# Norms by token tile, start-up transfers in pieces, and the third mixer's tables requested later, in an fp32 four-layer network on one core

## What is computed

```python
# first block: per layer
x = x + mixer(rmsnorm(x, norm_mix[i]))
x = x + ec_moe(rmsnorm(x, norm_ffn[i]))
x = rmsnorm(x, final_norm)
# second block: per layer
h = h + 0.5 * _swiglu(_rmsnorm(h, norm_ffn1[layer]), ...)
h = h + mixer(_rmsnorm(h, norm_mix[layer]), ...)
h = h + 0.5 * _swiglu(_rmsnorm(h, norm_ffn2[layer]), ...)
return _rmsnorm(h, norm_final)

def _rmsnorm(x, g):
    xf = x.astype(jnp.float32)
    y = xf * lax.rsqrt(jnp.mean(xf * xf, axis=-1, keepdims=True) + RMS_EPS)
    return (y * g.astype(jnp.float32)).astype(x.dtype)
```

## Time and profile before

| | |
|---|---|
| median of 3 runs | 1685.31 us (1683.67 to 1689.7) |
| the profiled execution | 1685.38 us |
| its span | 1683.6 us |
| mean granted TensorE clock | 0.94 of full speed |
| PE busy | 1451.5 us (86%) |
| PE weight loads | 1191.5 us (71%) |
| DVE busy | 877.3 us (52%) |
| ACT busy | 622.6 us (37%) |
| POOL busy | 29.9 us (2%) |
| DMA | 408.73 MB, mean 243 GB/s |

### The profile page before, as it was taken

The page is one execution under the profiler, slowest core; times in us unless marked ns, Lnnn a source line. Parts: engine busy times, 40 slices in busy tenths (PEclk is TensorE's granted clock), DMA queues, the critical chain, the costliest instruction groups (busy, mean ns, idle before and its releaser), DMA issues.

```text
span 1683.6 us, 27005 instructions
## 1 busy us (share of the span) xinstructions
PE 1451.5 (86%) x10956; PEld 1191.5 (71%) x10956; DVE 877.3 (52%) x1601; ACT 622.6 (37%) x1050; POOL 29.9 (2%) x40
## 2 busy tenths in 40 slices
PE   7987876678977666799998879999999998889998
PEld 6765432356654323599997559999899998789997
DVE  5564211157732111555556966555655559755555
ACT  5372110144711101444431354444444437654443
POOL 0000000001000000100000000000000000000000
PEclk9998978888989978899998899999999999999999
DMA  9717999994279999955452424554455462445510
GB/s 402 312 62 302 425 427 429 429 427 195 87 300 426 428 429 428 412 201 200 176 224 103 150 100 151 200 199 175 175 200 196 174 229 102 181 181 200 182 68 26
DMA packets 31026, 408.73 MB, mean 243 GB/s; under 512 B 3376, under 2 KB 5424, under 8 KB 6496
## 3 DMA queue, kind: packets, MB, share of 16 engines
q1 hardware_dynamic: 28496, 404.33, 60.5%
q10 hardware_dynamic: 2448, 3.24, 0.6%
HBM read 406.50 MB, written 1.06 MB: 242 GB/s over the span
## 4 chain that ended last, share of the span: by engine, by line
PE 61%; DMA 16%; issue 13%; DVE 8%; ACT 2%; POOL 0%; SPq 0%; DVEq 0%; POOLq 0%; ACTq 0%
DMA ring<-stream 16%; PE bank L1718 8%; PE bank L1722 7%; PE bank L1719 7%; PE bank L1749 7%; PE bank L639 5%; PE bank L1755 3%; PE bank L1520 3%; PE bank L1502 3%; PE bank L645 3%; PE bank L1852 2%; PE bank L590 2%; PE bank L617 1%; PE bank L1431 1%; PE bank L2068 1%
## 5 line engine op out<-in xcount | busy, mean ns | idle before, releaser
L508 DVE TENSOR_TENSOR unit_lo<-ring,unit_hi 128x1024 fp32r<-128x1024 f32 x324 | 394.7, 1224 | 323.5 <-ACT unit_hi L503 323.3
L503 ACT ACTIVATE unit_hi<-ring 128x1024 fp32r<-128x1024 f32 x324 | 341.9, 1062 | 449.5 <-PE bank L1722 282.9
L1718 PE MATMUL bank<-hT_hi,unit_hi 128*128 128x256 f32 x1408 | 341.0, 282 | 1.6 <-DVE norm_lo L442 1.5
L1719 PE MATMUL bank<-norm_lo,unit_hi 128*128 128x256 f32 x1408 | 339.3, 279 | 0.0
L1718 PEld LDWEIGHTS bank<-hT_hi,unit_hi 128*128 128x128 f32 x1408 | 268.4, 191 | 5.8 <-issue 2.3
L1719 PEld LDWEIGHTS bank<-norm_lo,unit_hi 128*128 128x128 f32 x1408 | 266.0, 189 | 3.1
L1722 PE MATMUL bank<-hT_hi,unit_lo 128*128 128x256 f32 x1408 | 193.0, 279 | 0.0
L1502 PE MATMUL bank<-ring,work 128*32 128x256 f32 x1856 | 128.2, 429 | 58.4 <-DMA ring<-stream 58.4
L1722 PEld LDWEIGHTS bank<-hT_hi,unit_lo 128*128 128x128 f32 x1408 | 177.1, 188 | 0.0
L1502 PEld LDWEIGHTS bank<-ring,work 128*32 128x32 f32 x1856 | 62.0, 120 | 117.8 <-DMA ring<-stream 74.8
L1749 PE MATMUL bank<-unit_hi,act_lo 128*128 128x512 f32 x336 | 131.9, 393 | 0.0
(11 more groups left out here) (290 smaller groups left out, 1887.9 us busy)
## 6 DMA issues: line engine op xcount, KB each, us to landing
ring<-stream SPq DMA_DIRECT2D x183, 2048.0 KB, 12.1
work<-ahead SPq DMA_DIRECT2D x4, 2048.0 KB, 10.2
kept_slot<-ahead SPq DMA_DIRECT2D x2, 2048.0 KB, 24.0
ahead<-ahead SPq DMA_DIRECT2D x2, 2048.0 KB, 13.3
work<-spread ACTq DMA_DIRECT2D x2, 1024.0 KB, 12.1
x<-x_in SPq DMA_DIRECT2D x1, 1024.0 KB, 5.0
...
```

The lines of the kernel that those rows point to most:

```text
L503: nc.scalar.activation(high_buf(name, u), raw_unit(name, u), ACT.Copy).then_inc(hi_done, 1)
L508: low = nc.vector.tensor_tensor(low_buf(name, u), raw_unit(name, u), high_buf(name, u).bitcast(F32), ALU.subtract)
L1718: nc.tensor.matmul(out, high[:, k, :], hT_hi[:, k, :], start=(k == 0), stop=False)
L1719: nc.tensor.matmul(out, high[:, k, :], norm_lo[:, k, :], start=False, stop=False)
```

## The change

Eight norms (n0, n2, n5 to n9, f1) work token tile by token tile. ACT adds epsilon and the two sums of tile 0 with two small activations, and signals POOL through a semaphore of its own (`row_power_in`); DVE sums tile 1 (`row_sums`). ACT squares both halves of tile 0 first (table ROWS), except in n6 and n9, which follow a projection and keep the order of HALVES. POOL does one power per tile. Tile 0 of `xn` is written half by ACT and half by DVE, then tile 1 likewise. PE transposes the eight pieces of tile 0 first, then those of tile 1 group by group. The FFNs' last products and adds, and those of moe0, are made in token-tile order; r_out joins TAILS. r_in's first two unit splits move ahead of n8 on ACT and DVE. At the start the constants are requested in two parts, `x` in two and slot 0 in four transfers. ACT requests the tables of the third mixer after its part of n5, and the first eight products of that mixer wait for the transposed groups one at a time. In the first attention PE's wait for `cat_lo` moves from before scores(2) to before the weighted sum of pair 0, and DVE's `cat_lo` moves behind the normalization of the first pair.

```diff
...
-                if m in LAST_ADDS and name in TAILS:
+                if m in LAST_ADDS and name in TAILS and name != "r_out":
...
+                    if name == "r_out" and u == 7:
+                        low_ready(pe, name, u)
+                        for t in range(NT):
+                            for kk in range(2):
+                                for left, right in ((left_hi, high), (left_lo, high), (left_hi, low)):
+                                    mm = nc.tensor.matmul(proj_bank(m, t)[:, 0:width],
+                                                          left[:, 2 * j + kk, t * P:(t + 1) * P], right[:, kk, 0:width],
+                                                          start=False, stop=(kk == 1 and right is low), skip_group_check=True)
+                            mm.then_inc(unit_used if t else tail_done, 1)
+                        continue
...
-        TAILS = ["a_out", "c_out", "ffn0", "s_out", "ffn1", "ffn2", "ffn3"]
+        TAILS = ["a_out", "c_out", "ffn0", "s_out", "ffn1", "ffn2", "r_out", "ffn3"]
...
+        ROW_NORMS = ("n0", "n2", "n5", "n6", "n7", "n8", "n9", "f1")
...
+        ROWS = [(0, slice(0, 512)), (0, slice(512, 1024)), (1, slice(0, 512)), (1, slice(512, 1024))]
...
+        ORDER = {0: ROWS, 2: ROWS, 6: ROWS, 7: HALVES, 8: ROWS, 9: ROWS, 10: HALVES, 11: ROWS}
...
-        def norm_act(act, p, name=None):
...
-            if STAGE_AFTER.get(name) in FOLLOWS_UNITS:
+        EARLY_STAGES = (*FOLLOWS_UNITS, "r_in")
+        def norm_act(act, p, name):
...
+            if stage in EARLY_STAGES:
...
-                    split_high(act, STAGE_AFTER[name], u)
+                    split_high(act, stage, u)
+            done = SQUARES[p][0]
...
-                t, cols = HALVES[i]
+                t, cols = ORDER[p][i]
+                at = SS + 2 * t + cols.start // 512
...
-                                     accum_out=stat[:, SS + i:SS + i + 1]).then_inc(sq_act, 1)
-            if STAGE_AFTER.get(name) not in (None, *FOLLOWS_UNITS):
+                                     accum_out=stat[:, at:at + 1]).then_inc(sq_act, 1)
+                done += 1
+                if i == 0:
+                    if p == 0:
+                        act.wait_ge(const_in, 32)
+                    act.wait_ge(sq_act, done)
+                    nc.scalar.activation(stat[:, SS:SS + 1], stat[:, SS:SS + 1], ACT.Identity,
+                                         bias=cc("eps")[:, 0:1]).then_inc(sq_act, 1)
+                    done += 1
+                if (t, cols) == ROWS[1]:
+                    act.wait_ge(sq_act, done)
+                    nc.scalar.activation(stat[:, MS:MS + 1], stat[:, SS + 1:SS + 2], ACT.Identity,
+                                         bias=stat[:, SS:SS + 1]).then_inc(row_power_in, 1)
+            if name == "f1":
+                return
+            late = stage is not None and stage not in EARLY_STAGES
+            act.wait_ge(power_out, POWERS[name] + 1)
+            nc.scalar.activation(xn[:, 0, 0:512], x[:, 0, 0:512], ACT.Copy, scale=stat[:, RS:RS + 1]).then_inc(xn_done[0], 1)
+            if late:
...
-                split_high(act, STAGE_AFTER[name], 0)
-            if name is not None:
-                act.wait_ge(power_out, POWERS[name] + 1)
-                xn_act(act, RS)
-                if STAGE_AFTER.get(name) not in (None, *FOLLOWS_UNITS):
-                    split_high(act, STAGE_AFTER[name], 1)
+                split_high(act, stage, 0)
+            act.wait_ge(power_out, POWERS[name + "b"] + 1)
+            nc.scalar.activation(xn[:, 1, 512:1024], x[:, 1, 512:1024], ACT.Copy,
+                                 scale=stat[:, RS + 1:RS + 2]).then_inc(xn_done[0], 1)
+            if late:
+                split_high(act, stage, 1)
...
-        def norm_root(v, p, name):
-            norm_sums(v, p)
-            v.wait_ge(power_out, POWERS[name] + 1)
+        def row_sums(v, p):
+            v.wait_ge(*X_SOURCE[p])
+            nc.vector.tensor_tensor_reduce(xn[:, 1, 512:1024], x[:, 1, 512:1024], x[:, 1, 512:1024], 1.0 / D, 0.0,
+                                           ALU.mult, ALU.add, stat[:, SS + 3:SS + 4]).then_inc(sq_dve, 1)
+            v.wait_ge(sq_act, SQUARES[p][0] + 4)
+            v.wait_ge(sq_dve, SQUARES[p][1] + 1)
+            nc.vector.scalar_tensor_tensor(stat[:, MS + 1:MS + 2], stat[:, SS + 2:SS + 3], EPS, stat[:, SS + 3:SS + 4],
+                                           ALU.add, ALU.add).then_inc(power_in, 1)
...
         def norm_dve(v, p, q):
-            stage = STAGE_AFTER.get(f"n{q}")
-            norm_root(v, p, f"n{q}")
-            xn_dve(v, RS)
-            if stage is not None and stage not in FOLLOWS_UNITS:
+            name, stage = f"n{q}", STAGE_AFTER.get(f"n{q}")
+            row_sums(v, p)
+            v.wait_ge(power_out, POWERS[name] + 1)
+            nc.vector.tensor_scalar(xn[:, 0, 512:1024], x[:, 0, 512:1024], stat[:, RS:RS + 1], None,
+                                    ALU.mult).then_inc(xn_done[1], 1)
+            v.wait_ge(power_out, POWERS[name + "b"] + 1)
+            nc.vector.tensor_scalar(xn[:, 1, 0:512], x[:, 1, 0:512], stat[:, RS + 1:RS + 2], None,
+                                    ALU.mult).then_inc(xn_done[1], 1)
+            if stage is not None and stage not in EARLY_STAGES:
...
-            if f"n{q}" not in SPLIT_TURNS:
-                turn_evac(v, 1, f"n{q}")
+            if name not in SPLIT_TURNS:
+                turn_evac(v, 1, name)
...
         def norm_pe(pe, q):
-            for half in range(2):
-                pe.wait_ge(xn_done[0], 2 * q + half + 1)
-                pe.wait_ge(xn_done[1], 2 * q + half + 1)
-                turn_pe(pe, f"n{q}", 2 * half, 2 * half + 2)
-            if f"n{q}" not in SPLIT_TURNS:
-                turns_out(pe, f"n{q}")
+            name = f"n{q}"
...
+            first, end = TURN_AT[name]
+            pe.wait_ge(xn_done[0], 2 * q + 1)
+            pe.wait_ge(xn_done[1], 2 * q + 1)
+            for g in range(first, end):
+                if g >= 4:
+                    pe.wait_ge(*TURN_DONE[g - 4])
+                for src, at, rows, cols in TURNS[g][0][0::2]:
+                    nc.tensor.transpose(bank[g % 4][0:rows, at:at + cols], src, ident)
+            for g in range(first, end):
+                pe.wait_ge(xn_done[1 - (g - first) // 2], 2 * q + 2)
+                for src, at, rows, cols in TURNS[g][0][1::2]:
+                    last = nc.tensor.transpose(bank[g % 4][0:rows, at:at + cols], src, ident)
+                last.then_inc(turned, 1)
...
         def final_norm(v):
...
-            norm_root(v, 11, "f1")
+            row_sums(v, 11)
...
+                v.wait_ge(power_out, POWERS["f1b" if t else "f1"] + 1)
...
                 turn_probs_pe(pe, name, i)
+                if i == 1 and name == "a":
+                    pe.wait_ge(*TURN_DONE[TURN_AT["cat_a"][0]])
...
                 norm_probs_dve(v, name, i)
+                if i == 0 and divided is not None:
+                    divided()
...
             def gated_turn():
                 turn_pe(pe, "cat_a")
-                pe.wait_ge(*TURN_DONE[TURN_AT["cat_a"][0]])
...
                 for i in range(4):
-                    half, t = divmod(i, 2)
+                    t, half = reversed(divmod(i, 2)) if l else divmod(i, 2)
...
                 for i in range(4):
-                    t, cols = HALVES[i]
+                    t, cols = HALVES[i] if l else ROWS[i]
...
-                    nc.vector.tensor_tensor(xs, bank[2 * t + i // 2][:, :], xs,
+                    nc.vector.tensor_tensor(xs, bank[2 * t + cols.start // 512][:, :], xs,
...
                     for i in range(4):
-                        half, t = divmod(i, 2)
+                        t, half = divmod(i, 2)
...
             for i in range(4):
-                t, cols = HALVES[i]
+                t, cols = ROWS[i]
...
-                nc.vector.scalar_tensor_tensor(xs, bank[2 * t + i // 2][:, :], 0.5, xs, ALU.mult,
+                nc.vector.scalar_tensor_tensor(xs, bank[i][:, :], 0.5, xs, ALU.mult,
...
                     for k in range(KD):
+                        if c == 0 and at == 0 and k % 2 == 0:
+                            pe.wait_ge(*TURN_DONE[TURN_AT["n5"][0] + k // 2])
...
         def _(sp):
-            sp.dma_start(x[:, :, :], x_in.rearrange("(t p) d -> p t d", p=P)).then_inc(x_loaded, 16)
-            sp.dma_start(con[:, :], consts).then_inc(const_in, 16)
-            first = PCOL["gains"][1]
+            first, early = PCOL["gains"][1], CCOL["eps"][1]
+            sp.dma_start(con[:, 0:early], consts[:, 0:early]).then_inc(const_in, 16)
...
-            for s in range(RING):
+            for t in range(NT):
+                sp.dma_start(x[:, t, :], x_in[t * P:(t + 1) * P, :]).then_inc(x_loaded[t], 16)
+            for u in range(4):
+                sp.dma_start(ring[:, 0, u * UNIT:(u + 1) * UNIT], stream[0, :, u * UNIT:(u + 1) * UNIT])\
+                  .then_inc(first_in[u] if u < 3 else slot_in[0], 16)
```

(5 more changed lines are left out.)

59 lines of the change are left out of this document (38 added, 21 removed).

## The result

The changed kernel takes 1688.76 us (median of 20 runs, 1685.27 to 1695.15), the kernel before 1686.42 (20 runs, 1683.67 to 1689.70). The ratio is 1.0018, with a 95% interval of 1.0010 to 1.0026: slower by 0.18%, where 0.8% faster was forecast. The profiled execution has a span of 1688.8 us, 5.2 more than before.

A forecast was written before the change was run, and what follows sets the result against it. PE was taken as the bound (61% of the last chain, 16% waiting for the weight stream). Terms 1.3 + 1.4 + 4.6 + 0.8 + 0.9 + 0.9 + 0.8 = 10.7 gave 1674.6 us; 2.6 from the clock, 1672.0; range 1669.5 to 1676.

The forecast's parts named there:

- does not touch the unit splits and products that fill the rest: Between stages: the change works only on PE's idle gaps, so the gain is at most a few us per boundary.
- half clock everywhere: Rival for every stage start: tile 0's short transpose burst leaves the clock low, costing 21.7 us, 1696.3 us; chance 0.04.
- the first product isn't earlier: Sign of being wrong, at the program's start: the first product was forecast near 12.3 us instead of 13.6.
- tile order gives nothing back: Rival at seven norm boundaries: ten transposes at half clock cost 1.1 us each, 7.7 in all, 1682.4 us; chance 0.13.
- Start, 1.3: Program start: split transfers and less ACT work bring the first product from 13.6 to 12.3 us, gaining 1.3 (0 to 2.0).
- Attention, 1.4: First attention: scores(2) no longer wait for `cat_lo` and DVE normalizes pair 0 earlier, gaining 1.4 us (0.6 to 1.9).
- n5, 4.6: Norm n5 and third mixer: later table requests and group-by-group waits start its products earlier, gaining 4.6 us (4.2 to 5.1).
- n2 0.4, n6 0.3, n7 0.1, n8 0.9, n9 0.9: Gains in us at the other norms, from tile order and, at n8, from r_in's split moved ahead of the norm.
- End, 0.8: Kernel's end: tile 0's power is ready early, so DVE's scaling of it starts sooner, gaining 0.8 us (0 to 1.24).
- The small activations, nothing: In the norms: sixteen small activations and eight POOL powers cost nothing; on the path, 0.4 us each, 3.0 in all.
- The clock, 2.6 taken back: Half-clock stretches after n2, n5 and n9 cost 6.5 us; shorter PE gaps were to return two fifths, 2.6 us.
- Gains ahead of the first expert stage move its stream forward: First expert stage: its weight stream resumes when the first mixer frees slots, so time won ahead of it counts.

The follow-up runs named there:

- E2: The kernel before with 8 unused columns at the end of `con`, moving `work` by 32 bytes, no instruction changed: 1696.11 us, 1.0064 of before.
- E1: The changed kernel with table `half` cut from 32 to 24 columns, so `work` lies at the address of before: 1678.97 us, 0.9964 of before.
- E3: The changed kernel itself measured once more, on the chip of E1 and E2: 1689.86 us, 1.0029 of before.
- E12: E1 itself measured once more, beside E11 on the same chip: 1678.13 us, 0.9954 of before.
- E11: E1 with PE's transposes in group order again, so the first evacuation needs 4 transposes instead of 10: 1672.40 us, 0.9920 of before.
- E4: E1 with 8 unused columns ahead of `hT` and `half` cut by another 8: activations move 32 bytes, split weights stay; 1685.73 us, executed once.
- E7: The changed kernel with `work` at 64 mod 128 and the activations at 96 mod 128: 1679.76 us, 0.9960 of before.
- E9: E1 with the third mixer's part undone: table requests ahead of n5, PE waits for all four transposed groups; 1679.52 us, 0.9966 of before.
- E10: The kernel before with only the third mixer's part (later table requests, group-by-group waits), nothing moved in memory: 1682.37 us, 0.9975 of before.
- E8: The changed kernel with `work` at 64 mod 128 and the activations at 32 mod 128: 1683.16 us, executed once.

## Why the prediction was wrong

**The step that failed** is the sentence that the change "does not touch the unit splits and products that fill the rest". It costed what instructions do and not where their operands lie. The new constant moved the split weights by 32 bytes, to the same place mod 128 as the activations, and 4224 products became 3.0 ns slower, while 576 products of the projections became 6 ns faster: together a loss of 11.0 us by E2 and 10.9 by E1 against E3. None of the rivals had it. The one that ended slower (half clock everywhere, 1696) did not happen either: the changed kernel's mean granted clock was 0.946, that of before 0.94. One of the prediction's own signs of being wrong did show: the first product isn't earlier.

**The rest, term by term,** against E1 and E12, where the address is that of before. Their two ratios give gains of 6.1 and 7.8 us; the sum was 10.7, and 13.3 with the clock. A second assumption failed in several terms: that the ten transposes ahead of the first evacuation run at full clock, 0.12 us each. The rival "tile order gives nothing back" priced the half clock, and where it set in, the rival was right.

- *Start, 1.3:* 0.1 to 0.2. The pieces landed as forecast (ACT squares tile 0 at 5.69, DVE tile 1 at 6.99) and ACT's wait for slot 0 went. The Trainium skill's fixed 2.0 us for each transfer ("DMA: Bandwidth & Descriptors", section "Anatomy of one DMA", measured for transfers issued by GpSimd) did not add up over them: the trace disagrees with that reading, and the 4.0 us that it would have cost did not come. But ten transposes at half speed stood ahead of the first evacuation: it came 2.46 us behind the first transpose instead of 1.18, which is the whole term. The rival was right here. The clock has no record yet in this stretch, so its row did not show the slow step; the 3.31 us for 16 transposes in the timeline of before would have. (E11's expectation, with 0.235 us a transpose, took busy time over count; they start 0.21 apart.)
- *Attention, 1.4:* right, 1.3. The wait for `cat_lo` went, and from PE's first scores to the first product of a_out it is 28.4 us in before and 28.3 in E2, and 26.9 to 27.4 in the changed kernel, E1, E4 to E7, E9 and E12 (E1 27.1), each with one half-clock stretch of 3.4 us in it. Where the stretch is twice as long this doesn't show: 28.8 in E10, 28.3 in E8, 29.1 in E11. From the program's first product on, the gain is hidden in E12 (96.7 us to a_out, before 96.1, E1 94.8), because its first ten products run at half speed, 0.2 us each too slow.
- *n5, 4.6:* right, 5.2 where the clock stayed up and about 4 in E3, where it did not. E10 shows that it belongs to the requests and the waits.
- *n2 0.4, n6 0.3, n7 0.1, n8 0.9, n9 0.9:* in E1 0.6, -0.3, 0.1, -0.2 and 1.1. The two losses are the rival again, ten transposes at half clock. Where the clock stayed up, n6 gave 0.7 (changed; 0.4 against E2) and n8 0.9 (E3), as forecast or better; n7 at half clock, in the changed kernel, lost 1.0. *End, 0.8:* 0.6 (from DVE's last sum to its first scaling 1.77 before, 1.21 in E1).
- *The small activations, nothing:* not so. They lie between ACT's squares, which start 0.95 us apart (1195.38 and 1196.33 in the changed kernel) instead of 0.63 and hold back tile 0, and POOL's two powers queue behind one another. By the timeline that is why tile 0 was not the 1.2 us ahead that I had assumed; no run tries it by itself.
- *The clock, 2.6 taken back:* the half-clock stretch after n5 is also shorter in E2, with the instructions of before: from the mixer's first product to its next stage 51.7 us as in E1, against 54.0. I had read one execution's stretches as a cost of the kernel. Such a term can't be taken from one profile. The idle gaps did shrink nearly as forecast, to 2.70 in n5 and 2.81 in n7 and n8, and half clock still set in behind n7, n8 and n9 (windows of the changed kernel; the columns are those of the earlier trace rows):

```profile
1198.00:1203.00 5.00, 3.52 (x16) 0.66 0.00 0
1393.00:1404.00 11.00, 8.99 (x42) 0.53 0.00 0
1489.00:1496.00 7.00, 5.66 (x28) 0.51 0.20 75
```

  The Trainium skill ("TensorE: Matmul & The Clock Gate", section "Why this matters for your kernels") wants such gaps short; the trace agrees behind n5 and n6, where the clock stayed up, and not behind these three. In E3, the same kernel with the same gaps (2.70 and 2.23), half clock set in behind n5 and n6 and not behind n8 (2.81), so the length of the gap alone did not decide it.
- *Gains ahead of the first expert stage move its stream forward:* they did not show. The last product before n2 ends between 351.7 and 354.7 in before, E2 and E10, and between 352.3 and 356.9 in the changed kernel, E1, E3 and E12. E1 is 1.5 us ahead of before at the first product of a_out and 0.26 at this point. E12's profile is 4.65 us behind E1's at that point and 5.4 at the end, with the same program: of the difference between these two, most arises before that point.

Terms as measured in E1, start and attention with the 0.3 that is left of them behind the first expert stage: 0.3 + 0.6 + 5.2 - 0.3 + 0.1 - 0.2 + 1.1 + 0.6 = 7.4, between the two measured gains. With -10.9 for the address this is a loss of 3.5; measured were 2.3 in the first comparison and 4.8 in E3's.
